# The latent tiles' queries and scores of layer 0 spread over two gather jobs, with the six-slot ring kept through both

## The reference, cut to what matters

```
q  = (xb @ w_q)                      # 8 heads x 256
s1 = q[first 128 of a head] . keys[0]   # 128 scores a head
s2 = q[last 128 of a head]  . keys[1]   # 128 scores a head
v1,i1 = top16(s1);  v2,i2 = top16(s2)
pos of the best 16 among the 256 sums v1+v2  ->  expert index i1*128 + i2
g   = softmax(best 16 sums)
act = gelu(u_tab[expert] . x)
out = sum over 8 heads x 16 experts of  g * act * v_tab[expert]
```

## Time and profile before

| | before |
|---|---|
| median of 3 runs | 4455.33 us (4454.01 to 4455.74) |
| profiled execution | 4460.96 us |
| its span, first to last instruction | 4459.2 us |
| mean granted TensorE clock | 0.863 |
| TensorE, VectorE, ScalarE, GpSimd busy | 71%, 62%, 38%, 34% |
| HBM read | 1531 MB, of it gathers 1342 MB |

### The profile page before, as it was taken

The page is one execution under the profiler, slowest core; times in us unless marked ns, Lnnn a source line. Parts: engine busy times, 40 slices in busy tenths (PEclk is TensorE's granted clock), DMA queues, the critical chain, the costliest instruction groups (busy, mean ns, idle before and its releaser), DMA issues.

```text
span 4459.2 us, 71818 instructions
## 1 busy us (share of the span) xinstructions
PE 3187.5 (71%) x26519; PEld 1573.3 (35%) x26519; DVE 2772.4 (62%) x7117; ACT 1708.1 (38%) x5328; POOL 1495.1 (34%) x1298
## 2 busy tenths in 40 slices
PE   7978788869866558765667776786786687666555
PEld 4534577443321114431323432352452153132111
DVE  1256644266657766776656776766676776665764
ACT  1036322033323334543325563554563363332332
POOL 0000000024344444443434444443444443443443
PEclk9997799889987779897888998898998898888777
DMA  5162000189999999999999999999999999999998
GB/s 224 52 239 88 15 7 5 58 321 405 417 392 421 421 421 417 420 417 409 419 420 410 419 419 408 418 417 399 415 419 420 417 419 414 417 417 420 412 420 333
DMA packets 238220, 1538.85 MB, mean 345 GB/s; under 512 B 33222, under 2 KB 34337, under 8 KB 67505
## 3 DMA queue, kind: packets, MB, share of 16 engines
q0 software_dynamic: 184768, 1342.45, 72.9%
q1 hardware_dynamic: 52664, 191.69, 11.2%
q10 hardware_dynamic: 442, 0.12, 0.0%
HBM read 1531.06 MB, written 3.10 MB: 344 GB/s over the span
## 4 chain that ended last, share of the span: by engine, by line
DMA 49%; PE 13%; DVE 7%; ACT 5%; issue 3%; POOL 2%; SPq 0%; ACTq 0%; POOLq 0%; PEldq 0%; DVEq 0%
DMA t_ring<-in_peer_uv,t_eidx 47%; PE t_ps L2217 8%; DVE t_ring L1691 5%; POOL t_ring L1565 2%; PE t_ps L2044 1%; PE t_ps L2114 1%; ACT t_dg L1859 1%; ACT t_wgt L1853 1%; ACT t_wgt L1848 1%; DMA t_wg<-in_cv_w_pw 1%; DMA t_wq<-in_cv_w_pw 1%; PE t_ps L2218 0%; PE t_ps L2155 0%; PE t_ps L2132 0%; ACT t_early L1888 0%
## 5 line engine op out<-in xcount | busy, mean ns | idle before, releaser
L1565 POOL DMA_INDIRECT t_ring<-in_peer_uv,t_eidx x1280 | 1487.6, 1162 | 2930.5 <-PE t_ps L2220 1849.1
L2217 PE MATMUL t_ps<-t_ring,t_dg 64*64 64x512 f32 x2560 | 1557.4, 739 | 1029.7 <-ACT t_dg L1859 1002.0
L1691 DVE SCALAR_TENSOR_TENSOR t_ring<-t_ring,t_hring 128x1024 f32<-128x1024 f32 x1024 | 1255.6, 1226 | 818.8 <-DMA t_ring<-in_peer_uv,t_eidx 816.1
L2220 PE MATMUL t_ps<-t_ring,t_dg 64*64 64x512 f32 x2560 | 1575.7, 747 | 0.0
L2219 PE MATMUL t_ps<-t_ring,t_dg 64*64 64x512 f32 x2560 | 1575.3, 747 | 0.0
L2218 PE MATMUL t_ps<-t_ring,t_dg 64*64 64x512 f32 x2560 | 1574.8, 746 | 0.0
L2217 PEld LDWEIGHTS t_ps<-t_ring,t_dg 64*64 64x64 f32 x2560 | 341.6, 154 | 1964.0 <-issue 1929.6
L1848 ACT ACTIVATE t_wgt<-t_dots 128x2 f32<-128x2 f32 x640 | 130.3, 204 | 1926.8 <-DVE t_ring L1691 1926.1
L1691 DVE SCALAR_TENSOR_TENSOR t_ring<-t_ring,t_early 128x1024 f32<-128x1024 f32 x256 | 314.6, 1229 | 248.7 <-DMA t_ring<-in_peer_uv,t_eidx 248.2
L1859 ACT ACTIVATE t_dg<-t_eye,t_wgt 128x64 f32<-128x64 f32 x1280 | 376.3, 340 | 1.8 <-ACT t_wgt L1853 1.1
L2220 PEld LDWEIGHTS t_ps<-t_ring,t_dg 64*64 64x64 f32 x2560 | 342.7, 155 | 0.0
(11 more groups left out here) (363 smaller groups left out, 4416.9 us busy)
## 6 DMA issues: line engine op xcount, KB each, us to landing
t_wq<-in_peer_w_q SPq DMA_DIRECT2D x112, 512.0 KB, 7.9
ev_mod_ring<-in_mod_w SPq DMA_DIRECT2D x48, 1024.0 KB, 9.5
t_wg<-in_cv_w_pw SPq DMA_DIRECT2D x48, 512.0 KB, 8.5
t_ring<-in_peer_uv,t_eidx POOLq DMA_INDIRECT x1280, 14.0
t_wq<-in_cv_w_pw SPq DMA_DIRECT2D x40, 512.0 KB, 9.0
ev_wring<-in_ab_w_in SPq DMA_DIRECT2D x21, 512.0 KB, 3.7
ev_qk<-in_ab_w_out SPq DMA_DIRECT2D x1, 4096.0 KB, 12.4
t_lrow<-modrows SPq DMA_DIRECT2D x6, 512.0 KB, 17.3
```

The lines of the kernel that those rows point to most:

```text
L1565: pool.indirect_dma_start(ring[:, place[n], :], None, table, bass.IndirectOffsetOnAxis(ap=eidx[:, s % 2, r:r + 1], axis=0)).then_inc(row_i ...
L1691: V.scalar_tensor_tensor(ring[:, place[n], 0:D], ring[:, place[n], 0:D], 1.0, h_of(j), ALU.mult, ALU.mult, accum_out=dots[:, j % 2, r:r + ...
L2217: nc.tensor.matmul(straight[low], diagonal[low], row[low, 0:512], **ends)
L2220: nc.tensor.matmul(crossed[low], diagonal[high], row[high, 512:D], **ends).then_inc(S["used"], 1)
```

## The change

It makes five edits.

- `place`: the first 256 picks (jobs 0 and 1) use six slots, and the last two are taken from pick 256 on.
- `score_tick`: a table of 17 ticks counted over jobs 0 and 1. Blocks 0 to 7 start in job 0, blocks 8 to 15 and the last scores (entry 16) in job 1, at 132 and later.
- `qT0` moves to the place of `hT1`.
- TensorE and ScalarE make the latents' generator once, before the loop over jobs, and run it with the tick counted over the jobs.
- SP issues job 0's gate row before the weight blocks of the queries.

```diff
-    place = [n % (R - 2) if n < PICKS else (R - 2 + n - PICKS) % R for n in range(JOBS * PICKS)]
+    place = [n % (R - 2) if n < 2 * PICKS else (R - 2 + n - 2 * PICKS) % R for n in range(JOBS * PICKS)]
-    score_tick = lambda b: 26 + 2 * (11 * b // 4)
+    score_tick = lambda b: (40, 50, 60, 70, 80, 95, 110, 118, 132, 138, 145, 151, 158, 164, 171, 177, 184)[b]
-        qT0 = early[:, 6144:6144 + 2 * T_LAT].rearrange("p (a t) -> p a t", a=2)
+        qT0 = early[:, 8672:8672 + 2 * T_LAT].rearrange("p (a t) -> p a t", a=2)
 # SP
+                for _ in gate_row(0, 0):
+                    pass
                 for n in range(Q0):
                     load_q(0, n % NC, n)
...
-                    sides = [Side(gate_row(j, 14)) for j in (0, 1, NT, NT + 1) if s == j]
+                    sides = [Side(gate_row(j, 14)) for j in (1, NT, NT + 1) if s == j]
 # ScalarE
+                latents = Side(latent_scores())
...
-                        sides += [context, Side(latent_scores())]
+                        sides.append(context)
...
                         run_sides(sides, 2 * c)
+                        latents.run(s * PICKS + 2 * c)
                         weigh(s, c)
 # TensorE
+                latents = Side(score_latents())
...
-                    sides = [context, Side(score_latents())] if s == 0 else []
+                    sides = [context] if s == 0 else []
...
                         run_sides(sides, 2 * c)
+                        latents.run(s * PICKS + 2 * c)
```

## The result

The changed kernel took 4466.69 us (median of 8 runs) against 4454.67 for the kernel before in the same comparison: ratio 1.0027, 95% interval 1.0018 to 1.0036, some 12 us slower. The forecast was 4451.9 in a range of 4445 to 4462 and was wrong; the time is that of the rival "cold blocks run six slots dry" (4466.6), which had 0.13. The profiled execution took 4469.8 us, its span 4468.0.

A forecast was written before the change was run, and what follows sets the result against it. Expert-row gathers saturating DMA at 421 GB/s were taken as the bound, so only dry moments or moved bytes count. Terms -3.1 - 1.2 + 0.1 + 0.8 = -3.4 us from 4455.33 gave 4451.9, range 4445 to 4462.

The forecast's parts named there:

- cold blocks run six slots dry: Rival: first halves in job 0 cost 1.5 us each, 0.5 in job 1; +11.3 us, 4466.6, chance 0.13.
- The latent blocks: Blocks cost 0.5 us each in job 0, 0.15 in job 1, against 5.1 before; +0.1 us.
- Six slots through job 1: Six slots in job 1 carry 420 GB/s against 421; +0.8 us, bounds 0 and 4.7.
- The end of job 0: DMA's dry spell at 1296 to 1302 goes, -3.5 us; one late pair of picks stays, +0.4; together -3.1 us.
- the inversion: At job 0's end pick 130 waits for slot 0 while slots 2 to 5 come free earlier; 3.5 us lost.
- The gate row: Job 0's gate row moves from saturated time to nearly idle DMA ahead of the weight blocks; -1.2 us, bounds 0 and -2.7.
- Score waits: VectorE needs a head's scores four or five ticks after ScalarE copies them; no wait, 0 us, bound +3.
- SP's queue: Columns, job 1's gate row, layer-1 keys and gated-unit weights wait behind weight blocks, their bytes still in saturated time; 0 us.
- The signs that I named: Right: gate row first, no POOL wait over 7 us, job 0 at 410 GB/s; wrong: job 1 below 410.

The follow-up runs named there:

- c1: Changed kernel with blocks 0 to 7 back at the old ticks, 5.5 apart, blocks 8 to 15 left in job 1; ratio to the kernel before 0.9997.
- a1: Changed kernel with the tick table of before, all sixteen blocks in job 0, six slots still in both jobs; ratio to the kernel before 0.9991.
- b3: Kernel of before with only the change's ring edit, six slots through jobs 0 and 1; ratio to the kernel before 1.0003.
- o1: Kernel of before with only the slot order from pick 128 on changed to 6, 7, 2, 3, 4, 5, 0, 1; ratio 0.9990.
- b1: Kernel of before with job 0's gate row ahead of the weight blocks and slots from pick 128 in order 6, 7, 2, 3, 4, 5, 0, 1; ratio 0.9988.
- a3: Changed kernel with eight idle matmuls behind each pair of picks at which no half is due; ratio to the kernel before 0.9996.
- a4: Changed kernel with two idle matmuls behind each pair of picks at which no half is due; ratio to the kernel before 1.0019.

## Why the prediction was wrong, by its own steps

- **The latent blocks, +0.1 us (bounds -2.7 and +10.9): this step failed.** It took 0.5 us for each isolated block of job 0 "nearer to the second" of two starts. Measured by c1 against the change it is 1.7 us a block, 13 us, above even the upper price of 1.5; the whole term is 16 us by a1, outside its bounds. What I left out is the pair of picks ahead of the half, which is at half clock too and delays the slots as well, and the echo one ring round later. Pair and half together took 8.4 us at the dry start at 1018, and 7.2 at the one at 1062 that I leaned on (its pair's products took 0.61, 0.59, 0.77 and 1.05 us). But blocks of the change with the same 7.1 to 7.3 us fell to 379 to 397 GB/s, while that start kept 413 in the same 16 us; why it was so mild stays open, and it was no guide. The reason that I gave for discounting 1018 (the next half being two ticks off) held for every new block too: each has its second half two ticks behind the first. For job 1's blocks 0.15 each was too little by the trace (377 GB/s and 10.3 us lost in the 99 us ahead of the column loads), but by c1 against a1 they cost about 3 us in all.
- **Six slots through job 1, +0.8 us:** likely under-priced, but not shown. It is 6 us by b3 against o1, past the bound of 4.7, and 1.3 by a1 against b1; the traces have 7.5 and 2.6. I took 20 us of a quiet stretch (1276:1296) for the price of 332.
- **The end of job 0, -3.5 + 0.4:** the inversion is real and worth its price (o1: 4.5 us), and with six slots and nothing behind it the end costs the 0.5 that I took (b3). In the change it isn't won. The end still loses 3.1 us in 24 at a clock of 0.54. What stands there besides is block 8, four ticks into job 1. c1, which has the blocks of job 0 far from the end, still loses 2.6 us in the same 24, and b3, without block 8, only 0.5. With block 8 there and TensorE at full clock (a3, 1272 to 1296, clock 1.00) DMA moved 409 GB/s, 0.7 us lost. These are single traces.
- **The gate row, -1.2 us:** issued first, ahead of the weight blocks (timeline of SP below); its size lies under what a run shows.
- **Score waits, SP's queue:** 0 each, and nothing in the traces speaks against it. Of 258 us for which VectorE waits from 950 to 1641, 254.9 are for gathers, 1.5 for the join of the job's end, and none for the score copies. SP issues all 32 weight blocks until 1404.6, columns, row and keys by 1461, 180 us ahead of job 1's end.
- **The signs that I named:** no wait of POOL over 7 us near a job's end, and the gate row first, came true. Job 0 at 398 GB/s and not 410, the end of job 0 losing 3.1 us and not under 2, and job 1 at 377 ahead of the column loads spoke against it.

```profile
882.58 0.48 SPq L1521 DMA_DIRECT2D t_grow<-modrows  x1
883.11 521.48 SPq L1485 DMA_DIRECT2D t_wq<-in_peer_w_q  x32
1404.63 25.43 SPq L1538 DMA_DIRECT2D t_cols<-modrows  x4
```

The sum by what was measured: blocks +16 (a1 against the change, both jobs), six slots +1 to +6, inversion -4.5, gate row 0 to -1, together +11.5 to +17.5 where +12 was found. The blocks' 16 us are worked out from that same +12, so what this tests is the rest: a1 has the other terms alone and is 4 us under before, where they add up to -4.5 to +1.5.

The rival that came true named the place and nearly the price (1.5 us). That its total, 4466.6, meets the measured 4466.69 is luck in part: it had 10.9 us for the blocks where 16 were found, and counted on 3.1 us at the end of job 0 that weren't won. a3 and a4 show the clock at work in time and not only in its level: 0.84 to 0.98, 14 us. The Trainium skill ("TensorE: Matmul & The Clock Gate", section "HAM oscillation") advises, for matmuls with few rows, to do all of one tile's work before waiting for DMA, so that the engine stays at its high clock; these runs agree, for another shape of kernel. It had 0.13 because I counted one dry start against one full one and called it even; the 4.84 and 3.7 us of a cold half and a cold pair, added up as a delay against the slots' reserve, might have told more than the count.

## What to carry to other kernels

A ring that feeds a saturated DMA queue has a reserve in time, and here what ate it was the stretch in which the consumer gave nothing back. Spreading side work thins its mean but not that stretch. Here it made it longer: seven of eight lumps came behind a pair of picks that ran at half clock, three ran partly at half clock themselves. In such a kernel keep lumps close together, or pad between them, and price a lump with the unit of work ahead of it. Where a ring changes its size, write down for each slot which pick it waits for; where the consumer gives slots back in order, a slot reused out of order makes the producer wait for the youngest user (here one line, 4.5 us, interval 0.4 to 9).

## What was not expected of the hardware

Idle matmuls made the kernel faster: eight of 128 columns (2.05 us at full clock) behind a pair took the change from 1.0027 to 0.9996, while two (clock 0.89) took it to 1.0019 only. And the part ahead of the retrieval, which no version touched, ended anywhere between 876.4 and 898.7 us in the fourteen traces, 22 us, more than any effect studied here; what moves it was not looked into.
